# Who scales and shifts the last tile of H behind an inner norm: ScalarE or VectorE

## The chip, the cores and the metric

The kernel runs on one core of a Trainium2 chip (trn2). The metric is the device time of one execution in microseconds (us), as the median of several executions. Engines are called as the profile calls them: PE (TensorE; PEld are its weight loads), DVE (VectorE), ACT (ScalarE), POOL (GpSimd), SP (SyncE, which issues most of the loads).

## What is computed

One inference step of a backbone with two layers. Layer 0 mixes tokens by differential attention, layer 1 by a bidirectional mLSTM; each mixer is followed by a gated ConvFFN. 128 context tokens and 512 latent tokens go through together (640 columns), with 1024 features. Each of the four sub-layers ends in a post-norm, and the next sub-layer reads a modulated copy of its result. Cut to what matters here:

```python
def layer_norm(x, g, b):
    mu = jnp.mean(xf, axis=-1, keepdims=True)
    var = jnp.mean(jnp.square(xf - mu), axis=-1, keepdims=True)
    return (xf - mu) * lax.rsqrt(var + EPS) * g + b
def modulate(x, shift, scale):
    return x * (1 + scale) + shift
...
xs = post_norm(xs, mod_s[2] * ys, ln_g[i, 0], ln_b[i, 0])
hs = modulate(xs, mod_s[3], mod_s[4])
fs = conv_ffn(hs, ffn_w_up[i], ffn_conv_w[i], ffn_conv_b[i], ffn_w_down[i])
```

Shift and scale differ between context and latent tokens. Everything is float32.

## The kernel before, in words

Activations are kept feature-major: `X` holds 8 tiles (j = 0 to 7) of 128 features by 640 tokens. A float32 product is made of three products in fp32r: every operand is split into a high part (a cast) and a low part (the operand less its high part), and PE computes high·high, high·low of the weights, and low·high. So a tile of activations needs `Hh` (cast, by ACT) and `Hl` (subtraction, by POOL), and a unit of weights needs `whi` (ACT) and `wlo` (POOL).

The order on each engine is written out by hand, one program for each engine, and semaphores tie them together. There are three inner norms: norm 0 behind the attention's output projection, norm 1 behind the first ConvFFN, norm 2 behind the mLSTM's output projection. (The fourth, at the end, has no H behind it and isn't touched.) Around each of them:

- PE ends the statistics (`layer_norm_stats`, L658 to L668), and cannot go on until the first tile of H is there.
- DVE (`layer_norm`, L1728 to L1749) forms the variance, then for each j subtracts the mean (L1747) and multiplies by the reciprocal deviation (L1744), which leaves the normed `X[:, j]`, and raises `xn_ready`.
- ACT (`h_build`, L1142 to L1151) waits for `xn_ready`, computes gain times X plus bias into one of two buffers `h32[j % 2]` in two instructions (L1149: 128 columns with the context's `la` and `lb`, 512 with those of the latents), drains, and casts the buffer into `Hh[:, j]` (L1151), which raises `h_hi`. From j = 2 on it first waits for `h_ready`, that the low part of tile j - 2 has been made, so that its buffer is free.
- POOL (`h_lo`, L528 to L532) subtracts `Hh` from the buffer into `Hl[:, j]` and raises `h_ready`.
- PE (`first_pair`, L609 to L617, behind norms 0 and 2) runs, for each j, the high products of the first two weight units when `h_hi` has come (8 matmuls), and then the low ones when `h_ready` has come (4 matmuls). Behind norm 1 the place of the second unit is taken by the gates' columns (L920), also 12 matmuls for each j.

What follows on each engine: behind norms 0 and 2, DVE splits the third weight unit itself (`ffn`, L1765 `wnh` and L1767 `wnl`; `wnl` raises `w_lo`, for which SP waits before it loads the next unit into that buffer), behind norm 0 it also clears and fills `condf` (L1668, L1671), and then it starts the convolutions of the ConvFFN (L1753 to L1759). Behind norm 1 it fills two constants and two tiles of the identity (L1985 to L1989) and then waits for the gates. POOL goes on, behind norms 0 and 2, with the residual (L536) and the low parts of weights (L541). ACT empties the first two results (L1139) as soon as PE has ended them, and PE's third unit waits for the first of these copies.

Of the kernel before, what the change touches and what calls it, by code (L numbers as in the profile page):

```python
# [10 lines left out]
ALU = mybir.AluOpType  # L11
ACT = mybir.ActivationFunctionType
# [4 lines left out]
KT = D // P  # L17
# [56 lines left out]
LAST = KT - 1  # L74
# [13 lines left out]
SPANS = ((C0, C0 + CTX, 0), (L0, L0 + LAT, 1))  # L88
# [64 lines left out]
def hybrid_step(nc, a, o):  # L153

    ctx = ExitStack()
    with ctx:
        def sb(name, shape, dt=F32, scope=ctx):
            return scope.enter_context(nc.sbuf_tensor(name, shape, dt))
# [4 lines left out]
        def sem(name):  # L163
            return ctx.enter_context(nc.semaphore(name))


        X = sb("X", [P, KT, TP])
# [11 lines left out]
        la = sb("la", [P, KT, 2])  # L179
        lb = sb("lb", [P, KT, 2])  # L180
# [9 lines left out]
        h32 = [h32t[:, k, :] for k in range(2)]  # L190
# [125 lines left out]
        h32_ready, h_hi, h_ready = sem("h32_ready"), sem("h_hi"), sem("h_ready")  # L316
# [809 lines left out]
        def _(act):  # L1126
            fn = nc.scalar.activation
# [14 lines left out]
            def h_build(inst, n):  # L1142

                for j in range(KT):
                    act.wait_ge(xn_ready, KT * n + j + 1)
                    if j >= 2:
                        act.wait_ge(h_ready, KT * (n + 1) + j - 1)
                    for t0, t1, m in SPANS:
                        fn(h32[j % 2][:, t0:t1], X[:, j, t0:t1], ACT.Identity, scale=la[:, j, m:m + 1], bias=lb[:, j, m:m + 1])  # L1149
                    act.drain()  # L1150
                    nc.scalar.copy(Hh[:, j, :], h32[j % 2][:, :]).then_inc(h_hi, 1)  # L1151

            def square(n, j):
# [247 lines left out]
            acc_tiles(U_WO, 0, D, D, parted=True)  # L1401
            layer_norm(0)
            h_build(2, 0)
            ffn(0, U_FFN0, last=False)
            act.wait_ge(wg_in, 16)
            act.wait_ge(wg_clear, 1)
            for r, c in GCOL:
                last = nc.scalar.copy(wgh[:, :, r:r + 4], wgf[:, :, c:c + 4])
            last.then_inc(wgh_ready, 1)
            layer_norm(1)  # L1410

            h_build(3, 1)
            act.wait_ge(g_done, 1)
            fn(gr[0], mS[0:GR, :, 0:HALF], ACT.Identity, bias=gbias[0:GR, :])
# [210 lines left out]
            acc_tiles(U_MLOUT, 2, D, D, parted=True)  # L1625
            layer_norm(2)
            h_build(5, 2)
            ffn(1, U_FFN1, last=True)
            layer_norm(3)
# [9 lines left out]
        def _(dve):  # L1639
            tt, ts, stt = nc.vector.tensor_tensor, nc.vector.tensor_scalar, nc.vector.scalar_tensor_tensor  # L1640
# [87 lines left out]
            def layer_norm(n):  # L1728

                dve.wait_ge(va_done, n + 1)  # L1730
                dve.wait_ge(musq_ready, n + 1)
                sx2 = sx[:, 0:TP].rearrange("p (a b) -> p a b", a=2)
                stt(out=sx2, in0=rs[:, :, :], scalar=-1.0, in1=st_va[:, :, 0:HALF], op0=ALU.mult, op1=ALU.add)
                dve.drain()
                ts(sx[:, 0:TP], sx[:, 0:TP], 0.0, EPS, ALU.max, ALU.add).then_inc(var_ready, 1)
                if n == 3:
                    nc.vector.tensor_copy(ss[:, :].rearrange("p (a b) -> p a b", a=2), st_mu[:, :, 0:HALF]).then_inc(mur_ready, 1)
                tiles = KT if n < 3 else SIDE[0]
                for j in range(tiles + LEAD):
                    if j == LEAD:  # L1740
                        dve.wait_ge(rstd_psum, n + 1)
                    if j >= LEAD:
                        x = X[:, j - LEAD, :].rearrange("p (a b) -> p a b", a=2)
                        tt(x, x, st_va[:, :, 0:HALF], ALU.mult).then_inc(xn_ready, 1)  # L1744
                    if j < tiles:
                        x = X[:, j, :].rearrange("p (a b) -> p a b", a=2)
                        tt(x, x, st_mu[:, :, 0:HALF], ALU.subtract)  # L1747
                    if j > 0:
                        dve.drain()  # L1749

            def conv(c, f, tap, bias):

                ts(c[:, :], f[:, :], tap[1], bias, ALU.mult, ALU.add)  # L1753
                dve.drain()
                for t0, t1 in ((C0, L0), (L0, TP)):
                    stt(out=c[:, t0 + 1:t1], in0=f[:, t0:t1 - 1], scalar=tap[0], in1=c[:, t0 + 1:t1], op0=ALU.mult, op1=ALU.add)  # L1756
                dve.drain()
                for t0, t1 in ((C0, L0), (L0, TP)):
                    last = stt(out=c[:, t0:t1 - 1], in0=f[:, t0 + 1:t1], scalar=tap[2], in1=c[:, t0:t1 - 1], op0=ALU.mult, op1=ALU.add)  # L1759
                return last  # L1760
# [192 lines left out]
            for w in range(2):  # L1953
                dve.wait_ge(kv_out[w], 16 * DA_HEADS)
            layer_norm(0)
            ffn(0, U_FFN0)
            def gate_columns():
# [21 lines left out]
            for r, c in GCOL:  # L1979
                last = tt(wgl[:, :, r:r + 4], wgf[:, :, c:c + 4], wgh[:, :, r:r + 4].bitcast(F32), ALU.subtract)  # L1980
            last.then_inc(wg_ready, 1)
            layer_norm(1)


# [221 lines left out]
            coefficients((1, 0), mod(1, 3), mod(1, 4))  # L2206
            gated(U_MLOUT, NMOD + 2 * KT, True)
            layer_norm(2)
            dve.wait_ge(c_out, 32 * ML_HEADS)
            ffn(1, U_FFN1)  # L2210
# [97 lines left out]
```

## Time and profile before

| what | value |
|---|---|
| median of 3 executions | 1843.4 us (1843.14 to 1843.87) |
| the profiled execution, its own time | 1841.11 us |
| span of its trace | 1839.3 us |
| mean granted TensorE clock | 0.978 of full speed |
| PE busy | 1725.6 us, 94% of the span |
| PEld busy | 1613.5 us, 88% |
| DVE busy | 1050.2 us, 57% |
| ACT busy | 694.4 us, 38% |
| POOL busy | 642.7 us, 35% |

The span is what the trace covers; the execution's own time is 1.8 us more. Busy shares are averages over the whole program. In a timeline each row is one instruction, or a run of alike ones (x2), with its start in us from the span's start, its duration, its engine, its line in the kernel, the tiles written and read, and in brackets how long the engine was idle before and what ended that.

### The profile page before, as it was taken

The page shows a single profiled execution, that of the slowest core. Times are in us where ns is not written, and L with a number is a line of the kernel's source. Part 1 is how long each engine was busy: PE and PEld are TensorE (multiplying, and loading weights), DVE is VectorE, ACT ScalarE, POOL GpSimd, SP SyncE. Part 2 cuts the span into 40 slices and gives each one's busy share as a digit, 9 for nine tenths or more (in the row PEclk, how much of TensorE's full clock was granted, in tenths as well). Part 3 has the DMA queues.
Part 4 walks back from the last instruction along what each step waited for, and adds up shares of the span by engine and source line. Part 5 has one row for each costly group of instructions (what it writes and reads, how often), then busy time and mean ns, then how long its engine had stood idle before and what let it go on. Part 6 is the DMA issues. An engine that isn't in the chain of part 4 may idle for free.

```text
span 1839.3 us, 29894 instructions
## 1 busy us (share of the span) xinstructions
PE 1725.6 (94%) x11444; PEld 1613.5 (88%) x11444; DVE 1050.2 (57%) x1651; ACT 694.4 (38%) x1074; POOL 642.7 (35%) x292
## 2 busy tenths in 40 slices
PE   6899999788999999999978999997989999999996
PEld 3688888588988999899977999996979999999996
DVE  1277767755765614667337544544568881387823
ACT  3255555534423212322236544644253331133323
POOL 3312221335533333333435222222555333233444
PEclk8999999888999999999999999999999999999998
DMA  9722122111355223453211111110212222122221
GB/s 378 261 70 68 53 69 68 32 35 58 139 185 191 75 80 109 153 202 123 81 64 41 47 58 58 49 56 18 69 46 80 70 96 69 63 69 80 82 79 57
DMA packets 54034, 169.35 MB, mean 92 GB/s; under 512 B 7728, under 2 KB 13232, under 8 KB 53936
## 3 DMA queue, kind: packets, MB, share of 16 engines
q1 hardware_dynamic: 47600, 163.79, 26.0%
q10 hardware_dynamic: 6336, 4.20, 0.8%
q8 instruction: 69, 1.13, 0.3%
q14 instruction: 29, 0.24, 0.0%
HBM read 159.04 MB, written 4.72 MB: 89 GB/s over the span
## 4 chain that ended last, share of the span: by engine, by line
PE 82%; DVE 7%; ACT 4%; DVEq 2%; issue 2%; DMA 2%; POOL 1%; ACTq 0%; SPq 0%; POOLq 0%
PE pj L601 69%; PE mO L999 2%; DMA awr<-in_w_ada 2%; PE psO L777 2%; PE psS L742 1%; PE pfrow L626 1%; PE psT L758 1%; DVE pr L1856 1%; ACT pr L1260 1%; POOL X L549 1%; DVE sm L1841 1%; PE mS L955 1%; PE prow L626 1%; DVE h32t L1877 1%; PE mT L1024 1%
## 5 line engine op out<-in xcount | busy, mean ns | idle before, releaser
L472 POOL TENSOR_TENSOR wlo<-wraw,whi 128x1024 fp32r<-128x1024 f32 (+1 forms) x130 | 334.0, 2570 | 827.4 <-ACT whi L1134 827.4
L601 PE MATMUL pj<-Hh,whi 128*128 128x320 f32 x2400 | 569.7, 319 | 44.8 <-issue 13.7
L601 PE MATMUL pj<-Hh,wlo 128*128 128x320 f32 x2400 | 552.0, 312 | 0.0
L601 PE MATMUL pj<-Hl,whi 128*128 128x320 f32 x2400 | 546.3, 311 | 1.0 <-POOL Hl L502 1.0
L601 PEld LDWEIGHTS pj<-Hh,whi 128*128 128x128 f32 x2400 | 402.2, 190 | 76.8 <-issue 51.4
L601 PEld LDWEIGHTS pj<-Hh,wlo 128*128 128x128 f32 x2400 | 406.7, 190 | 0.0
L601 PEld LDWEIGHTS pj<-Hl,whi 128*128 128x128 f32 x2400 | 404.1, 190 | 1.3 <-POOL Hl L502 1.3
L1134 ACT CAST whi<-wraw 128x1024 fp32r<-128x1024 f32 (+1 forms) x180 | 199.4, 1108 | 314.2 <-PE pj L601 277.1
L1756 DVE SCALAR_TENSOR_TENSOR fcv<-fus,vec,fcv 128x127 f32<-128x127 f32 (+1 forms) x176 | 231.8, 1358 | 15.6 <-issue 15.6
L1711 DVE SCALAR_TENSOR_TENSOR X<-pj,mods,X 128x128 f32<-128x128 f32 (+1 forms) x144 | 54.5, 434 | 268.5 <-PE pj L601 268.2
L601 PE MATMUL pj<-Gh,wlo 128*128 128x320 f32 x704 | 160.4, 309 | 0.0
L601 PE MATMUL pj<-Gh,whi 128*128 128x320 f32 x704 | 160.4, 309 | 0.0
L601 PE MATMUL pj<-Gl,whi 128*128 128x320 f32 x704 | 160.3, 309 | 0.0
L1139 ACT COPY fus<-pj 128x640 f32<-128x640 f32 x88 | 60.7, 692 | 223.4 <-PE pj L601 223.2
L1759 DVE SCALAR_TENSOR_TENSOR fcv<-fus,vec,fcv 128x127 f32<-128x127 f32 (+1 forms) x176 | 123.6, 743 | 15.1 <-issue 15.1
L510 POOL TENSOR_TENSOR wlo<-wraw,whi 128x1408 fp32r<-128x1408 f32 (+2 forms) x28 | 83.9, 2995 | 105.5 <-ACT whi L1134 101.7
L601 PEld LDWEIGHTS pj<-Gl,whi 128*128 128x128 f32 x704 | 117.7, 188 | 0.0
L601 PEld LDWEIGHTS pj<-Gh,wlo 128*128 128x128 f32 x704 | 117.7, 188 | 0.0
L601 PEld LDWEIGHTS pj<-Gh,whi 128*128 128x128 f32 x704 | 117.6, 188 | 0.0
L1753 DVE TENSOR_SCALAR fcv<-fus,vec 128x640 f32<-128x640 f32 x88 | 58.8, 668 | 102.2 <-ACT fus L1139 102.1
L1218 ACT CAST Gh<-fpr 128x640 f32 (+1 forms) x44 | 32.0, 728 | 214.2 <-DVE fpr L1783 214.2
L541 POOL TENSOR_TENSOR wlo<-wraw,whi 128x1024 fp32r<-128x1024 f32 x24 | 59.2, 2470 | 126.6 <-ACT whi L1134 126.6
(306 smaller groups left out, 2046.2 us busy)
## 6 DMA issues: line engine op xcount, KB each, us to landing
wraw<-in_w_up SPq DMA_DIRECT2D x88, 512.0 KB, 3.3
fwr<-in_w_ada SPq DMA_DIRECT2D x56, 512.0 KB, 5.7
wraw<-in_w_dn SPq DMA_DIRECT2D x32, 704.0 KB, 4.0
awr<-in_w_ada SPq DMA_DIRECT2D x40, 512.0 KB, 10.3
wraw<-in_w_qkv SPq DMA_DIRECT2D x24, 512.0 KB, 3.5
wraw<-in_w_mlin SPq DMA_DIRECT2D x24, 512.0 KB, 3.2
sx<-h32t SPq DMA_DIRECT2D x128, 32.0 KB, 2.0
wraw<-in_w_wo SPq DMA_DIRECT2D x8, 512.0 KB, 3.3
```

The lines of the kernel that those rows point to most:

```text
L472: nc.gpsimd.tensor_tensor(wlo[k][:, 0:width], wraw[k][:, 0:width], whi[k][:, 0:width].bitcast(F32), ALU.subtract).then_inc(w_lo, 1)
L510: nc.gpsimd.tensor_tensor(wlo[k][:, c0:width], wraw[k][:, c0:width], whi[k][:, c0:width].bitcast(F32), ALU.subtract).then_inc(w_lo, 1)
L541: nc.gpsimd.tensor_tensor(wlo[v % 2][:, 0:width], wraw[v % 2][:, 0:width], whi[v % 2][:, 0:width].bitcast(F32), ALU.subtract).then_inc(w_l ...
L601: last = mm(out[:, c, 0:HALF], w, x[:, j, c * HALF:(c + 1) * HALF], start=(j == 0 and n == 0), stop=(j == n_k - 1 and n == 2))
L626: last = mm(out[g:g + 32, :], conds[:, 2 * kp + r, PAD - 2 * b:PAD - 2 * b + 32], bufs[u % len(bufs)][:, r, :], start=(b == 0 and kp < 2), ...
L777: last = mm(psO[:, :], v_[par][:, c, :], t_[:, c, :], start=(c == 0 and n == 0), stop=(c == 4 and n == 2))
L1134: nc.scalar.copy(whi[k][:, 0:width], wraw[k][:, 0:width]).then_inc(w_hi, 1)
L1139: nc.scalar.copy(dst.rearrange("p (a b) -> p a b", a=2), pj[k if pairs == 2 else 0][:, :, 0:HALF]).then_inc(pj_copied, 1)
L1711: last = stt(out=x, in0=pj[k][:, bank, c0:c1], scalar=gt, in1=x, op0=ALU.mult, op1=ALU.add)
L1753: ts(c[:, :], f[:, :], tap[1], bias, ALU.mult, ALU.add)
L1756: stt(out=c[:, t0 + 1:t1], in0=f[:, t0:t1 - 1], scalar=tap[0], in1=c[:, t0 + 1:t1], op0=ALU.mult, op1=ALU.add)
L1759: last = stt(out=c[:, t0:t1 - 1], in0=f[:, t0 + 1:t1], scalar=tap[2], in1=c[:, t0:t1 - 1], op0=ALU.mult, op1=ALU.add)
```

## The change

Behind each of the three inner norms, the scaling and shifting of the last tile (`LAST` = 7) is taken out of ACT's program and put into DVE's, behind the last multiplication of the norm. DVE waits for `h_ready` of tile 5, whose buffer `h32[1]` it overwrites, issues one tensor_scalar for each of the two spans, and raises the semaphore `h32_ready`, which existed and was not used. ACT waits for that in place of its two instructions and its drain, and casts as before.

```diff
                     if j >= 2:
                         act.wait_ge(h_ready, KT * (n + 1) + j - 1)
-                    for t0, t1, m in SPANS:
-                        fn(h32[j % 2][:, t0:t1], X[:, j, t0:t1], ACT.Identity, scale=la[:, j, m:m + 1], bias=lb[:, j, m:m + 1])
-                    act.drain()
+                    if j == LAST:
+                        act.wait_ge(h32_ready, n + 1)
+                    else:
+                        for t0, t1, m in SPANS:
+                            fn(h32[j % 2][:, t0:t1], X[:, j, t0:t1], ACT.Identity, scale=la[:, j, m:m + 1], bias=lb[:, j, m:m + 1])
+                        act.drain()
                     nc.scalar.copy(Hh[:, j, :], h32[j % 2][:, :]).then_inc(h_hi, 1)
...
                     if j > 0:
                         dve.drain()
+                if n < 3:
+                    dve.wait_ge(h_ready, KT * (n + 1) + LAST - 1)
+                    for t0, t1, m in SPANS:
+                        last = ts(h32[LAST % 2][:, t0:t1], X[:, LAST, t0:t1], la[:, LAST, m:m + 1], lb[:, LAST, m:m + 1], ALU.mult, ALU.add)
+                    last.then_inc(h32_ready, 1)
```

The instructions of DVE behind norm 0, before (wnh and wnl are the high and low part of the third weight unit, st_mu and st_va hold mean and reciprocal deviation):

```order
L1747 TENSOR_TENSOR X<-X,st_mu 128x640
L1744 TENSOR_TENSOR X<-X,st_va 128x640 x2
L1765 TENSOR_SCALAR wnh<-wraw 128x1024
L1767 TENSOR_TENSOR wnl<-wraw,wnh 128x1024
L1668 MEMSET condf 128x496
L1671 COPY condf<-cond 128x8x2
```

And now; the first of the two new ones waits for `h_ready`:

```order
L1747 TENSOR_TENSOR X<-X,st_va 128x640 x2
L1756 TENSOR_SCALAR h32t<-X,la,lb 128x128
L1756 TENSOR_SCALAR h32t<-X,la,lb 128x512
L1773 TENSOR_SCALAR wnh<-wraw 128x1024
L1775 TENSOR_TENSOR wnl<-wraw,wnh 128x1024
L1671 MEMSET condf 128x496
L1674 COPY condf<-cond 128x8x2
```

Everything behind the two new instructions, the split of the third unit first, now stands behind the wait for POOL's tile 5. The same engine behind norm 1, now (vc, gnb: constants; mKh, mKl: the identity's tiles), where the same two rows have come ahead of four that don't touch H:

```order
L1747 TENSOR_TENSOR X<-X,st_va 128x640 x2
L1756 TENSOR_SCALAR h32t<-X,la,lb 128x128
L1756 TENSOR_SCALAR h32t<-X,la,lb 128x512
L1993 MEMSET vc 128x2
L1994 MEMSET gnb 128x1
L1996 TENSOR_SCALAR mKh<-ident 128x128
L1997 TENSOR_SCALAR mKl<-ident 128x128
```

ACT's last tiles behind norm 0, before (fus: the first two results of PE on their way to the convolution):

```order
L1149 ACTIVATE h32t<-X,lb,la 128x128
L1149 ACTIVATE h32t<-X,lb,la 128x512
L1151 CAST Hh<-h32t 128x640
L1149 ACTIVATE h32t<-X,lb,la 128x128
L1149 ACTIVATE h32t<-X,lb,la 128x512
L1151 CAST Hh<-h32t 128x640
L1139 COPY fus<-pj 128x640 x2
```

And now:

```order
L1152 ACTIVATE h32t<-X,lb,la 128x128
L1152 ACTIVATE h32t<-X,lb,la 128x512
L1154 CAST Hh<-h32t 128x640 x2
L1139 COPY fus<-pj 128x640 x2
L1134 CAST whi<-wraw 128x1024
```

The two casts stand next to each other, with a wait for DVE between them. The orders of PE, POOL and SP are the same in both kernels.

## Rows read from the trace of the kernel before

**Rows 1.** The page: the chain that ended last, by engine.

```profile
PE 82%; DVE 7%; ACT 4%; DVEq 2%; issue 2%; DMA 2%; POOL 1%; ACTq 0%; SPq 0%; POOLq 0%
```

**Rows 2.** The chain in order of time: start, us, what; around norms 0 and 2.

```profile
444.12 6.92 issue
451.04 16.73 PE pj L601 x94
468.68 28.46 PE pj L601 x192
...
1349.58 16.35 PE pj L601 x94
```

**Rows 3.** Busy time and granted clock in two stretches of first_pair behind norm 0.

```profile
451.00:457.00 6.00, 5.96 (x22) 5.99 (x23) 5.70 (x9) 5.81 (x11) 4.99 (x4) 0.50 0.01 3
457.00:468.60 11.60, 11.05 (x75) 10.78 (x74) 7.14 (x8) 7.74 (x14) 9.16 (x6) 1.00 0.14 46
```

**Rows 4.** Timeline of weight loads (PEld) behind norm 0, tiles 6 and 7.

```profile
464.22 0.34 PEld L601 LDWEIGHTS pj<-Hh,whi 128*128 128x128 f32 x2
...
465.98 0.33 PEld L601 LDWEIGHTS pj<-Hh,whi 128*128 128x128 f32 x2
...
467.15 0.63 PEld L601 LDWEIGHTS pj<-Hl,whi 128*128 128x128 f32 x4
```

**Rows 5.** Timeline behind norm 0, the other engines, tiles 5 to 7 and after.

```profile
459.76 0.95 DVE L1765 TENSOR_SCALAR wnh<-wraw 128x1024 fp32r<-128x1024 f32 x1 [0.16 <-issue]
...
460.48 1.66 POOL L532 TENSOR_TENSOR Hl<-h32t,Hh 128x640 fp32r<-128x640 f32 x1 [0.33 <-ACT Hh L1151]
460.80 2.42 DVE L1767 TENSOR_TENSOR wnl<-wraw,wnh 128x1024 fp32r<-128x1024 f32 x1
...
462.24 1.20 ACT L1149 ACTIVATE h32t<-X,lb,la 128x128 f32<-128x128 f32 x2
462.38 3.80 POOL L532 TENSOR_TENSOR Hl<-h32t,Hh 128x640 fp32r<-128x640 f32 x2 [0.23 <-ACT Hh L1151]
463.25 0.33 SPq L363 DMA_DIRECT2D wraw<-in_w_up  x1
...
463.50 0.73 ACT L1151 CAST Hh<-h32t 128x640 fp32r<-128x640 f32 x1
...
467.84 1.29 ACT L1139 COPY fus<-pj 128x640 f32<-128x640 f32 x2 [3.61 <-PE pj L601]
468.74 0.61 DVE L1753 TENSOR_SCALAR fcv<-fus,vec 128x640 f32<-128x640 f32 x1 [4.05 <-ACT fus L1139]
```

**Rows 6.** Timeline of norm 1, tiles 6 and 7 and what follows.

```profile
976.53 1.56 POOL L532 TENSOR_TENSOR Hl<-h32t,Hh 128x640 fp32r<-128x640 f32 x1 [0.32 <-ACT Hh L1151]
...
977.62 0.73 ACT L1151 CAST Hh<-h32t 128x640 fp32r<-128x640 f32 x1
...
978.43 1.56 POOL L532 TENSOR_TENSOR Hl<-h32t,Hh 128x640 fp32r<-128x640 f32 x1 [0.34 <-ACT Hh L1151]
...
979.14 0.31 PEld L920 LDWEIGHTS mS<-Hh,wgh 128*100 128x100 f32 x2
...
980.31 0.32 PEld L920 LDWEIGHTS mS<-Hl,wgh 128*100 128x100 f32 x2
```

**Rows 7.** Timeline behind norm 2, tiles 6 and 7.

```profile
1360.92 3.83 POOL L532 TENSOR_TENSOR Hl<-h32t,Hh 128x640 fp32r<-128x640 f32 x2 [0.22 <-ACT Hh L1151]
...
1362.06 0.73 ACT L1151 CAST Hh<-h32t 128x640 fp32r<-128x640 f32 x1
...
1364.15 0.33 PEld L601 LDWEIGHTS pj<-Hh,whi 128*128 128x128 f32 x2
...
1365.32 0.63 PEld L601 LDWEIGHTS pj<-Hl,whi 128*128 128x128 f32 x4
```

**Rows 8.** The page: group of the convolutions' first instruction, with its idle time.

```profile
L1753 DVE TENSOR_SCALAR fcv<-fus,vec 128x640 f32<-128x640 f32 x88 | 58.8, 668 | 102.2 <-ACT fus L1139 102.1
```

**Rows 9.** Timeline of ACT: the next use of the buffer that SP reloads.

```profile
479.18 1.05 ACT L1134 CAST whi<-wraw 128x1024 fp32r<-128x1024 f32 x1
```

## The prediction

> **What bounds the kernel now.** I read the chain that ended last first, because the change can only pay where it touches that chain. PE holds 82% of it, ACT 4%, POOL 1% [rows 1]. Then the same chain in order of time around the norms. Behind norm 0 there is a gap of 6.92 us in which PE waits for the norm, and from 451.04 on the chain is PE alone for 16.73 us, until ACT empties the first result and PE goes on at 468.68; behind norm 2 the run is 16.35 us [rows 2]. ACT's work on H is in neither stretch. That is worth a question, since ACT needs about 1.9 us for a tile (two instructions 1.20 us, a gap of 0.06, the cast 0.73, less a small overlap [rows 5]), and PE less: its loads for tile 6 begin at 464.22 and those for tile 7 at 465.98, 1.76 us apart [rows 4]. PE is the faster one and still never waits for ACT. The granted clock says why: from 451 to 457 us it was 0.50 (1.2 GHz), from 457 on 1.00 (2.4 GHz) [rows 3], after the idle gap. In the slow stretch PE fell behind ACT, and in the five tiles that follow it doesn't catch up fully.
>
> The last view is the timeline at the last tile, where I compare when a part of H is there with when PE first loads weights for it. These differences are the slack that a faster or slower tile 7 meets:
>
> - Norm 0: the cast ends at 463.50 + 0.73 = 464.23 [rows 5], PE wants it at 465.98 [rows 4]: slack 1.75 us. The low part ends at 462.38 + 3.80 = 466.18 [rows 5], wanted at 467.15 [rows 4]: slack 0.97.
> - Norm 1: the cast ends at 978.35, wanted at 979.14: slack 0.79. Low part 979.99, wanted 980.31: slack 0.32 [rows 6].
> - Norm 2: the cast ends at 1362.79, wanted at 1364.15: slack 1.36. Low part 1364.75, wanted 1365.32: slack 0.57 [rows 7].
>
> All six are positive, so an earlier tile 7 gains nothing. What is left to ask is whether the change can make it later than the slack.
>
> **What leaves ACT.** Two instructions and a drain per norm: about 1.20 + 0.06 = 1.26 us [rows 5], three times. ACT then waits 3.61 us for PE before it copies the first result [rows 5], so this time only makes that wait longer. Value on the path: 0.
>
> **What comes to DVE.** Two tensor_scalar with per-partition operands, 128 and 512 columns. The nearest row is the convolution's, the same kind with 640 columns: 0.61 us [rows 5]. The pair handles the same 640 columns with a second start, so I take 0.75 us (bounds: 0.61, and twice that, 1.22). When do they start? POOL's tile 5 began at 460.48 and took 1.66 us [rows 5], 1.56 when nothing disturbs it [rows 6]. What disturbed it was wnh, which ran until 460.71 and now stands behind it, so `h_ready` comes near 462.04. With 0.10 us for the signal (ACT was released by the same event: 462.14, then 462.24 [rows 5]) the pair runs from 462.14 to about 462.9, the cast until about 463.7. Against 464.23 it is some 0.5 us earlier, into slack. Value: 0.
>
> **The shared resource.** DVE and POOL don't run side by side here. wnl, 1024 columns, was issued at 460.80 and took 2.42 us; POOL's tile 5 ended at 462.14, and wnl 1.08 us after that. In the other direction, POOL's tiles 6 and 7 took 3.80 us in place of 2 x 1.56 = 3.12: tile 6, issued at 462.38, got going only as wnl ended [rows 5]. So one stands still while the other runs, and the new pair falls just where POOL starts tile 6 (462.38). The second instruction, that of 512 columns, starts near 462.4 (the first one's share of 0.75 behind 462.14). There are two orders, and both are worked out:
>
> - *DVE first.* POOL's tile 6 waits until about 462.8 and ends near 464.3, wanted at about 465.4 (464.22 and the 1.17 us that lie between PE's first high and first low load of a tile, 465.98 to 467.15 [rows 4]). wnh waits for tile 6 too. If it then goes before POOL's tile 7 (0.56 us of its 0.95 were work: POOL's tile 4 ended 0.33 before 460.48, at 460.15, and wnh at 460.71 [rows 5]), tile 7 ends near 464.85 + 1.56 = 466.4, still ahead of 467.15. Norm 1: tile 6 ends near 978.4, tile 7, with the identity's tiles in between, near 980.2, ahead of 980.31 by a hair. Norm 2: near 1364.9, ahead of 1365.32. Cost: 0, with 0.1 or 0.2 us possible in norm 1.
> - *POOL first.* This is the rival below.
>
> The Trainium skill, SBUF — State Buffer, section Who interferes with whom, says that a VectorE tensor_scalar in a 2-port mode and a GpSimd instruction take an exclusive lock, that "whoever issues first gets the shared pair for the whole instruction", and that the other blocks. By it the 512-column instruction could stand a whole POOL tile behind, which speaks against this change; the trace agrees with the rule in the 2.42 us above, and the result would be the rival's time below and not mine.
>
> **What is moved behind the wait.** wnh and wnl. PE needs them, with the first result emptied, at 468.68 [rows 2]. Before they were done at 460.80 + 2.42 = 463.22. Now, with DVE first: tile 7 of POOL ends near 466.4, wnl 1.08 us later, near 467.5; with wnh behind tile 7 as well it is much the same. Slack left 1.2 us; norm 2 has about 0.9. Cost 0; if the cover went, PE would wait by as much as wnl is later than 468.68. SP's next load into that buffer goes out at 463.25 [rows 5], now near 467.5. ACT reads the buffer at 479.18 [rows 9], 11.7 us later, so 0. POOL's residual waits for the same semaphore and moves by 1.3 us; nobody waits for it there. The copy into condf and the residual may push the first convolution, 468.74 [rows 5], back by 0.3 us, or by some 1.5 where POOL's next split then gets in ahead. DVE has idle time for this: 102.2 us in front of 88 convolutions, 1.16 us each [rows 8], and PE's two result buffers lie between. Cost 0.
>
> **The sum.** 0 from ACT, 0 from the earlier tile, 0 from the moved split: 1841.11 + 0 for an execution like the profiled one. The profiled one was 2.3 us below the median of 1843.4, so one execution can lie that far off; I put the change, 0, on the median: 1843.4 us.
>
> **Rivals.**
> 1. *PE does wait for ACT.* The ends of matmuls are modelled, and if PE in truth kept step with ACT at full clock, the last tile's two instructions would come off the path. For: ACT's 1.9 us for a tile exceed PE's 1.76 [rows 4, 5]. Against: the six slacks. At most the 0.5 us by which the cast comes earlier in norm 0, and 0.73 where it follows the cast before it at once: 3 x 0.73 = 2.2 us, 1841.2 us.
> 2. *POOL takes tile 6 first* (slower). Place: between `h_ready` of tile 5 and the 512-column instruction. POOL's tile 6 runs from 462.38 to 463.94, then DVE's instruction until about 464.3, the cast until 465.0 (wanted 465.98, fine). But now wnh and wnl are issued at once behind it, from 464.3 to about 466.1, while POOL's tile 7 can only be issued at 465.1, after the cast. It waits and ends near 466.1 + 1.56 = 467.65, 0.5 us late. Norm 2 by the same steps: tile 6 to 1362.48, wnl to 1364.6, tile 7 to about 1366.1, 0.8 late. Norm 1 has no wnl, but the least slack: tile 6 to 978.09, cast to 979.25, tile 7 from 979.3 to 980.87, 0.56 late. Together 1.9 us: 1845.3 us. It decides when the 512-column instruction comes to the port after POOL's tile 6, a matter of 0.1 us. For: the two times, 462.4 and 462.38, can't be told apart by rows. Against: POOL's tile 6, issued at 462.38 with wnl until 463.22 in its way, lost 0.68 us and not 0.84, so it wants the port some 0.15 us after its start, which favours DVE.
> 3. *The late wnl starts a chain* (clearly slower). PE waits for wnl, and a late first convolution never catches up: one whole POOL tile more per ConvFFN norm, 2 x 1.56 = 3.1 us, with the 1.9 above 5.0 us, 1848.4 us. Against: 1.2 and 0.9 us of slack and DVE's idle time.
>
> That the change doesn't do what it says is excluded by the order of the instructions.
>
> **How the numbers follow.** My forecast 0.60; rival 2, in one or more norms, 0.28; rival 1 0.06; rival 3 0.03; 0.03 for what I don't see. The range takes in rival 2 and a little of rival 1, and the 0.7 us by which executions differ: 1841.6 to 1845.6 us. A measurement of this kernel tells about 0.2% (3.7 us) from no change. Forecast and rivals 1 and 2 are all within that; only rival 3 and unseen things lie outside: faster 0.02, same 0.94, slower 0.04.
>
> **What would show it.** Right: PE's run behind each norm has the length it had (16.7 and 16.4 us), ACT's last cast ends near 463.7 in norm 0's time, POOL's tile 6 is issued at the old place and takes about 0.4 us longer than 1.56, wnl ends before PE's third unit. Wrong: a gap in PE ahead of the low products of tile 7 (rival 2), a shorter run with the cast in the chain (rival 1), PE released by wnl (rival 3).

## The result, and the profile after

| | before | after |
|---|---|---|
| median of 20 executions each, us | 1842.3 (1839.26 to 1844.46) | 1844.61 (1840.31 to 1848.93) |
| ratio after / before, 95% | | 1.0016 [1.001, 1.0022] |
| the profiled execution, own time / span, us | 1841.11 / 1839.3 | 1840.64 / 1838.9 |
| mean granted clock in it | 0.978 | 0.979 |

The change costs 0.16%, some 2.9 us (0.0016 x 1842.3; by the interval 1.8 to 4.1; the two medians lie 2.3 us apart). That is inside the 0.2% that the prediction called "no change" and inside its range, but 20 executions of each kernel do tell it from nothing: it is slower. The forecast's own mechanism, a cost of 0, is wrong. The two profiled spans say the opposite (0.4 us shorter), so nothing can be read off a span here: in four executions of the unchanged kernel, norm 0 alone starts anywhere from 442.17 to 445.96 us, for reasons that lie ahead of it. (One of the 12 executions of the last run below, e8, took 2225.32 us at a mean granted clock of 0.715 and is left out of its ratio.)

The page after the change, its busy times and the shares of the chain that ended last:

```profile
PE 1722.8 (94%) x11444; PEld 1610.0 (88%) x11444; DVE 1052.9 (57%) x1657; ACT 691.3 (38%) x1068; POOL 642.7 (35%) x292
...
PE 79%; DVE 7%; ACT 5%; DVEq 3%; DMA 2%; POOL 2%; issue 2%; ACTq 1%; SPq 0%; POOLq 0%
```

ACT's busy time fell by 3.1 us, as the change says. DVE's rose by 2.7, but between two executions of the unchanged kernel it already differs by 2.2 (1050.2 and 1052.4). The shares of the chain (PE 82% before [rows 1]) say that something else than PE now stands in it. The chain in order of time, around norms 0, 1 and 2 (start, us, what), shows what:

```profile
458.31 1.59 POOL Hl L532
460.02 2.04 DVEq L1774
462.96 2.42 POOL Hl L532
467.20 28.45 PE pj L601 x192
...
973.15 1.58 POOL Hl L532
974.76 2.15 DVE h32t L1756 x2
977.81 1.57 POOL Hl L532
...
1357.70 1.59 POOL Hl L532
1359.46 2.01 DVEq L1774
1362.38 2.43 POOL Hl L532
1366.36 218.61 PE pj L601 x1488
```

Behind each norm PE's unbroken run [rows 2] is gone. In its place stand POOL's tile 5, then DVE (DVEq L1774 is DVE's queue, which stands at the drain between wnh and wnl while the new pair runs), then POOL's tile 7. The timeline behind norm 0, the rows that answer to [rows 5]:

```profile
458.31 1.58 POOL L532 TENSOR_TENSOR Hl<-h32t,Hh 128x640 fp32r<-128x640 f32 x1 [0.32 <-ACT Hh L1154]
...
459.92 2.13 DVE L1756 TENSOR_SCALAR h32t<-X,la,lb 128x128 f32<-128x128 f32 x2 [2.53 <-POOL Hl L532]
...
460.20 1.57 POOL L532 TENSOR_TENSOR Hl<-h32t,Hh 128x640 fp32r<-128x640 f32 x1 [0.31 <-ACT Hh L1154]
...
461.97 0.68 DVE L1773 TENSOR_SCALAR wnh<-wraw 128x1024 fp32r<-128x1024 f32 x1
...
462.16 0.73 ACT L1154 CAST Hh<-h32t 128x640 fp32r<-128x640 f32 x1 [2.04 <-DVE h32t L1756]
462.74 1.23 DVE L1775 TENSOR_TENSOR wnl<-wraw,wnh 128x1024 fp32r<-128x1024 f32 x1
462.94 0.56 PE L601 MATMUL pj<-Hh,whi 128*128 128x320 f32 x2 [0.20 <-ACT Hh L1154]
462.96 2.40 POOL L532 TENSOR_TENSOR Hl<-h32t,Hh 128x640 fp32r<-128x640 f32 x1 [1.20 <-ACT Hh L1154]
...
465.42 0.85 PE L601 MATMUL pj<-Hl,whi 128*128 128x320 f32 x4 [1.04 <-POOL Hl L532]
...
467.20 0.54 PE L601 MATMUL pj<-Hh,wnh 128*128 128x320 f32 x2 [0.92 <-ACT fus L1139]
```

Read from the top. DVE is released at 459.92, 0.03 us behind the end of POOL's tile 5 (459.89). Its pair then takes 2.13 us and ends at 462.05, while POOL's tile 6, issued at 460.20, takes an undisturbed 1.57 and ends at 461.77. Taken singly, the two instructions of the pair are

```profile
459.92 0.35 DVE L1756 TENSOR_SCALAR h32t<-X,la,lb 128x128 f32<-128x128 f32 x1 [2.53 <-POOL Hl L532]
460.18 1.87 DVE L1756 TENSOR_SCALAR h32t<-X,la,lb 128x512 f32<-128x512 f32 x1
```

So the 128-column instruction went first, POOL's tile 6 came between the two, and the 512-column one had to wait for it, although its row begins at 460.18 and POOL's at 460.20: *POOL first*, the second of the two orders that the prediction worked out. The cast is late (PE waits 0.20 for it); behind it wnl (462.74 to 463.97) is in the port as POOL's tile 7 is issued, and that takes 2.40 in place of 1.56. PE waits another 1.04 us for the low part.

**The measure for the runs.** As spans don't help, I measure each norm by itself: from the start of DVE's variance instruction (L1733, a SCALAR_TENSOR_TENSOR into sx, at 444.33, 958.48 and 1342.87 in the profile before; L1736 in the changed kernel) to the start of PE's next unit behind the norm. From this start on, what DVE, ACT and POOL do in one kernel repeats in every execution within 0.05 us. A plus sign, as in +20.0, counts from this start too. Call it S.

| | norm 0 | norm 1 | norm 2 | sum |
|---|---|---|---|---|
| before, the profiled execution | 24.35 | 24.92 | 24.00 | 73.27 |
| after, the profiled execution | 25.06 | 25.46 | 24.80 | 75.32 |

Here the change costs 0.71, 0.54 and 0.80 us, 2.05 together. (The clock behind norm 0 was not the same in these two executions; see b1 below.)

### The profile page after: what moved, and what is told of

Read it like the earlier page. It is cut to its first block, busy times and chain, and to the rows that moved or that the text cites. A ratio compares the mean times of both kernels' runs of the same rounds, so it can differ in the third digit from the quotient of the medians.

```text
span 1838.9 us, 29891 instructions
## 1 busy us (share of the span) xinstructions
PE 1722.8 (94%) x11444; PEld 1610.0 (88%) x11444; DVE 1052.9 (57%) x1657; ACT 691.3 (38%) x1068; POOL 642.7 (35%) x292
## 3 DMA queue, kind: packets, MB, share of 16 engines
q8 instruction: 69, 1.13, 0.3%
## 4 chain that ended last, share of the span: by engine, by line
PE 79%; DVE 7%; ACT 5%; DVEq 3%; DMA 2%; POOL 2%; issue 2%; ACTq 1%; SPq 0%; POOLq 0%
PE pj L601 66%; PE mO L999 2%; DMA awr<-in_w_ada 2%; PE psO L777 2%; PE pfrow L626 1%; PE psS L742 1%; DVE pr L1864 1%; PE psT L758 1%; ACT pr L1263 1%; POOL X L549 1%; DVE sm L1849 1%; ACT Hh L1154 1%; PE mS L955 1%; ACT h32t L1152 1%; POOL Hl L532 1%
```

## The experiments

The theory (A) is **the port**: POOL's tile 6 gets in ahead of the 512-column instruction, and wnl, now late, gets in ahead of POOL's tile 7. Rivals: **the clock** (B), that the changed kernel's TensorE clock falls more often or stays low for longer, and that this is the time; and **the held queue**, that what costs is wnh and wnl behind the wait for POOL's tile 5, whoever does the scaling.

**Both kernels again.** No edit; the kernel before, then the one after.

> The kernel before, once more, against itself: this shows what two equal kernels differ by. Both theories: ratio 1.000, interval about 0.001 wide. Theory A (the port: the 512-column tensor_scalar is held up by POOL's tile 6 in every execution) says nothing on this run. Theory B (the loss comes from the TensorE clock, which the change lets fall more often) expects the granted clock of this kernel to be near 0.978 in all executions. A second question it answers: how long PE runs at the 1.2 GHz level behind each norm in another execution. In the profiled execution of before it was about 6 us behind norm 0, in that of the change about 3 us.

> The changed kernel once more. Theory A: ratio 1.0016 within 0.0008, and in the trace the pair of tensor_scalar takes 2.1 us in all three norms and POOL's tile 7 is issued 2.75 to 2.8 us after its tile 6. Theory B: the same ratio, but a granted clock that lies lower than that of before by 0.002 or more in most executions, with the PE gaps of about 1 us as its cause.

Measured: before against itself 1.0002 [0.9993, 1.0011], so with 11 executions against the runs of before nothing under 0.09% is told. After against before 1.0011 [1.0002, 1.002], 2.0 us, slower again. S before 24.32, 24.90, 23.99 (73.21); after 25.09, 25.48, 24.81 (75.38). The cost stands in S a second time, 2.17 us. The mean clock of the executions was 0.9781 for before and 0.9766 for after: the clock as a rival keeps a foothold that this doesn't settle (see the last point on the prediction, below).

**What the pair of instructions costs when POOL doesn't block it (e1).** DVE reads its second operand from PSUM and multiplies with it, in place of adding the bias, so the shift of tile 7 is left out; three instructions, since the PSUM tile has two banks.

```diff
-                    for t0, t1, m in SPANS:
-                        last = ts(h32[LAST % 2][:, t0:t1], X[:, LAST, t0:t1], la[:, LAST, m:m + 1], lb[:, LAST, m:m + 1], ALU.mult, ALU.add)
+                    for (t0, t1), (bk, c0, c1), m in (((0, 128), (0, 0, 128), 0), ((128, 320), (0, 128, 320), 1), ((320, 640), (1, 0, 320), 1)):
+                        last = stt(out=h32[LAST % 2][:, t0:t1], in0=X[:, LAST, t0:t1], scalar=la[:, LAST, m:m + 1], in1=st_va[:, bk, c0:c1],
+                                   op0=ALU.mult, op1=ALU.mult)
```

> DVE's instructions for tile 7 read a PSUM operand (X times gain times the reciprocal deviation, without the shift: the shift of tile 7 is left out and its values differ), so they have one SBUF input and no two-port mode. Everything else as in the changed kernel. Theory A: the three instructions take 1.1 us together in place of 2.1, ACT's last cast begins 0.9 to 1.0 us earlier after POOL's tile 5, POOL's tile 7 ends about 1.5 us earlier, PE has no gap over 0.3 us ahead of tile 7's low products; ratio 1.000 within 0.0006. Theory B without A (it is the handing over between engines that leaves the gaps, not the port): the instructions still end about 2.1 us after POOL's tile 5 and the ratio stays at 1.0016. Theory C (the moved split of the third unit is what costs): instructions short, but POOL's tile 7 as late as before, ratio over 1.001.

The timeline of this run behind norm 0:

```profile
461.53 1.13 DVE L1756 SCALAR_TENSOR_TENSOR h32t<-X,la,st_va 128x128 f32<-128x128 f32 x3 [2.51 <-POOL Hl L532]
461.81 1.57 POOL L532 TENSOR_TENSOR Hl<-h32t,Hh 128x640 fp32r<-128x640 f32 x1 [0.32 <-ACT Hh L1154]
...
462.57 1.36 DVE L1774 TENSOR_SCALAR wnh<-wraw 128x1024 fp32r<-128x1024 f32 x1
462.77 0.73 ACT L1154 CAST Hh<-h32t 128x640 fp32r<-128x640 f32 x1 [1.03 <-DVE h32t L1756]
463.58 1.78 POOL L532 TENSOR_TENSOR Hl<-h32t,Hh 128x640 fp32r<-128x640 f32 x1 [0.19 <-ACT Hh L1154]
...
464.03 2.42 DVE L1776 TENSOR_TENSOR wnl<-wraw,wnh 128x1024 fp32r<-128x1024 f32 x1
```

The three instructions take 1.13 us beside POOL's tile 6, which takes its 1.57: neither stops the other. The cast comes 1.00 us earlier than in the changed kernel (19.02 in place of 20.02 us behind the norm's start), and now it is POOL's tile 7 that comes first and wnl that waits (2.42). S: 23.43, 25.47, 23.85 (72.75); ratio 1.0006 [0.9997, 1.0015]. With the same wait, the same work moved off ACT and the same place on DVE, but without the port, the cost in S is gone behind norms 0 and 2 (1.63 and 0.95 us less than after). Behind norm 1 S is what it is after, but there the clock rose late (after 5.0 us), and the kernel before has 25.50 with such a clock (b1), so this norm tells nothing. The other two speak for the port and against the held queue. The ratio by itself doesn't: its interval holds both 1 and the 1.0011 of after. The Trainium skill (SBUF — State Buffer, section Who interferes with whom) says that a VectorE instruction with at most one SBUF input, outside the 2-port modes, does not contend with GpSimd, while one with two SBUF inputs does with a GpSimd instruction that reads SBUF; this form (1.13 us) and wnl (2.42) agree with it by these rows.

**The wait alone (e4).** DVE waits for tile 5 and then goes on with wnh; ACT scales tile 7 as before.

```diff
-                    if j == LAST:
-                        act.wait_ge(h32_ready, n + 1)
-                    else:
-                        for t0, t1, m in SPANS:
...
                     dve.wait_ge(h_ready, KT * (n + 1) + LAST - 1)
-                    for t0, t1, m in SPANS:
-                        last = ts(h32[LAST % 2][:, t0:t1], X[:, LAST, t0:t1], la[:, LAST, m:m + 1], lb[:, LAST, m:m + 1], ALU.mult, ALU.add)
-                    last.then_inc(h32_ready, 1)
```

> The kernel before (ACT still scales and shifts tile 7) with nothing but DVE's wait for POOL's tile 5 put ahead of what follows the norm on DVE: the moved split alone. Counted from the start of the variance (L1733), as in all traces. Theory A (the loss is the pair standing still behind POOL's tile 6, and then wnl on tile 7) expects ACT's last cast at +19.2 as before; wnh comes to the port at +17.8, ahead of tile 6, and wnl waits for tile 6 or for both; POOL's tile 7 ends between +21.6 and +22.7; PE's third unit behind norms 0 and 2 begins at +24.4 and +24.0 as before, or up to 0.3 later; ratio 1.000 to 1.0004. Theory C (the moved split is what costs): third unit at +25.0 and +24.8, ratio over 1.001.

```profile
463.81 0.69 DVE L1767 TENSOR_SCALAR wnh<-wraw 128x1024 fp32r<-128x1024 f32 x1 [2.51 <-POOL Hl L532]
...
464.09 4.36 POOL L532 TENSOR_TENSOR Hl<-h32t,Hh 128x640 fp32r<-128x640 f32 x2 [0.31 <-ACT Hh L1151]
...
464.60 2.42 DVE L1769 TENSOR_TENSOR wnl<-wraw,wnh 128x1024 fp32r<-128x1024 f32 x1
...
468.50 0.85 PE L601 MATMUL pj<-Hl,whi 128*128 128x320 f32 x4 [0.20 <-POOL Hl L532]
```

wnh, released at once, is in the port ahead of POOL's tile 6, and wnl (2.42 us) waits for tile 6 and then stands in front of tile 7: both tiles take 4.36 us, 1.24 above 2 x 1.56, where they took 3.80 before. S 23.95, 25.78, 23.98 (73.71), ratio 0.9999 [0.999, 1.0008]. The moved split by itself makes POOL 0.56 us later than before. Against the profile of before the sum of S is 0.44 us longer, but norm 1 alone is 0.86 longer, where no DVE instruction of this edit is in POOL's way (its clock rose late there, after 5.7 us). Norm 2, at the same clock as before, is unchanged (23.98 and 24.00); behind norm 0, at a clock between those of the executions of before (4.0 us), S lies between theirs and PE waits 0.20 us. So the held queue explains a few tenths behind norm 0 at most, not 2 us.

**wnl held back (e7).** The changed kernel; wnl waits until POOL's tile 7 is done, so only the second collision goes.

```diff
+                dve.wait_ge(h_ready, KT * (2 * layer + 2))
```

> The changed kernel, with wnl held back until POOL has made the low part of tile 7, so that it can't stand in its way. Theory A: the pair of tensor_scalar is as slow as before (2.13 us) and the last cast starts at +20.0, but POOL's tile 7 takes 1.57 us in place of 2.42 and ends at +22.4 in place of +23.2; PE's third unit begins at +24.3 to +24.4 behind norm 0 and +24.0 to +24.2 behind norm 2 (in place of 25.06 and 24.80), norm 1 stays at +25.46; ratio about 1.0005. If tile 7 still takes 2.4 us, wnl isn't what held it.

```profile
462.93 2.14 DVE L1756 TENSOR_SCALAR h32t<-X,la,lb 128x128 f32<-128x128 f32 x2 [2.51 <-POOL Hl L532]
463.21 1.58 POOL L532 TENSOR_TENSOR Hl<-h32t,Hh 128x640 fp32r<-128x640 f32 x1 [0.32 <-ACT Hh L1154]
...
465.99 1.58 POOL L532 TENSOR_TENSOR Hl<-h32t,Hh 128x640 fp32r<-128x640 f32 x1 [1.20 <-ACT Hh L1154]
467.60 1.23 DVE L1776 TENSOR_TENSOR wnl<-wraw,wnh 128x1024 fp32r<-128x1024 f32 x1 [1.92 <-POOL Hl L532]
467.62 0.85 PE L601 MATMUL pj<-Hl,whi 128*128 128x320 f32 x4
```

The first collision is unchanged (2.14), the second is gone: POOL's tile 7 takes 1.58, not 2.40. S 24.23, 25.47, 23.97 (73.67); ratio 1.0000 [0.9991, 1.0009]. Norms 0 and 2 get 0.83 us each back, norm 1, which has no wnl, nothing. The ratio's interval ends below that of the result (1.001), though it overlaps that of a0 (from 1.0002). So 1.7 us of the cost hang on wnl's place, behind a cast that the first collision has made late; the 0.5 us of norm 1 is the first collision alone.

**A third buffer (e2, and with wnl held e6).** Tile 7 goes to `sx`, which is free there, so that DVE needs no wait. In lines that the cut leaves out, ACT's cast and POOL's subtraction read `sx` for this tile, and ACT doesn't wait for tile 5 either; e6 adds e7's line.

```diff
-                    dve.wait_ge(h_ready, KT * (n + 1) + LAST - 1)
...
-                        last = ts(h32[LAST % 2][:, t0:t1], X[:, LAST, t0:t1], la[:, LAST, m:m + 1], lb[:, LAST, m:m + 1], ALU.mult, ALU.add)
+                        last = ts(sx[:, t0:t1], X[:, LAST, t0:t1], la[:, LAST, m:m + 1], lb[:, LAST, m:m + 1], ALU.mult, ALU.add)
```

> DVE writes tile 7 into a buffer of its own (sx, free at that time), so it waits for nobody, and neither ACT nor DVE waits for POOL's tile 5. ACT casts tiles 6 and 7 one behind the other. Theory A: DVE's pair falls beside POOL's tiles 4 and 5 and is done before ACT needs it, whoever has the port; POOL's tile 7 follows tile 6 at once and ends some 0.35 us earlier than in the kernel before, wnh and wnl stand where they stood or up to 1.5 us later; ratio 0.9995 to 1.0000 (3 x 0.35 = 1.0 us at most where PE keeps up with ACT). Theory B: about 1.000 too, as PE's gaps go. Theory C: over 1.001 if wnl falls on POOL's tile 7.

> A buffer of its own for tile 7 and wnl held back behind POOL's tile 7: what both findings suggest. Theory A: POOL's tiles 6 and 7 follow each other without hindrance and tile 7 ends at +21.2 to +21.3 in all three norms (before: 21.84, 21.51, 21.87). PE's third unit: no earlier than before where the clock stays at 1.2 GHz for over 5 us behind the norm (24.3 and 24.0), 0.3 to 0.6 earlier where it rises sooner. Ratio 0.9995 to 1.0003, which 5 rounds will hardly tell from 1.

The timeline of e2 behind norm 0:

```profile
459.30 1.58 POOL L532 TENSOR_TENSOR Hl<-h32t,Hh 128x640 fp32r<-128x640 f32 x1 [0.32 <-ACT Hh L1154]
...
460.39 1.03 DVE L1755 TENSOR_SCALAR sx<-X,la,lb 128x128 f32<-128x128 f32 x2
...
461.34 2.06 DVE L1772 TENSOR_SCALAR wnh<-wraw 128x1024 fp32r<-128x1024 f32 x1
...
463.50 2.43 DVE L1774 TENSOR_TENSOR wnl<-wraw,wnh 128x1024 fp32r<-128x1024 f32 x1
...
464.80 2.56 POOL L532 TENSOR_TENSOR Hl<-sx,Hh 128x640 fp32r<-128x640 f32 x1
```

The pair takes 1.03 us, and that isn't its size either: POOL's tile 4 runs until 460.88, and the 128-column instruction, issued at 460.39, takes 0.57 in place of 0.35. Unhindered the two take 0.35 (after) and 0.55 (e5 below), and their rows overlap by 0.08 or 0.09, so the pair is 0.81 us by itself. The last cast starts 17.88 us behind the norm's start (before: 19.17), yet POOL ends tile 7 at +22.3 (before +21.84) behind norms 0 and 2, since it and wnl collide again; that is not the earlier end that was expected. Behind norm 1, where there is no wnl, it ends at +21.15 (before +21.51). S of e2 24.65, 24.81, 23.97 (73.43), ratio 1.0006 [0.9997, 1.0015]; of e6, whose tile 7 takes 1.55 and ends at +21.31, 23.79, 25.87, 23.98 (73.64), ratio 1.0004 [0.9995, 1.0013]. An H that is ready 0.5 us earlier than before gives nothing that these runs can tell. (The high values of norm 1 in e4 and e6, 25.78 and 25.87, go with the latest clocks, 5.7 and 5.9 us.)

**The 512 columns first (e5).** The same two instructions in the other order; one execution.

```diff
-                    for t0, t1, m in SPANS:
+                    for t0, t1, m in SPANS[::-1]:
```

> The changed kernel with the two instructions of the pair in the other order. Theory A (whoever comes first has the port until its instruction ends): the 512-column one starts 0.03 us after POOL's tile 5, ahead of tile 6, and runs unhindered (about 0.5 us); POOL's tile 6 then goes and is itself 0.1 to 0.4 us longer than 1.57; the 128-column one waits for its end: the pair ends near +20.0 to +20.2, and the last cast starts no earlier than in the changed kernel (+20.0). If the port went to the shorter or to DVE by right, the pair would take 0.8 us and the cast start at +18.7.

```profile
463.57 2.06 DVE L1756 TENSOR_SCALAR h32t<-X,la,lb 128x512 f32<-128x512 f32 x2 [2.51 <-POOL Hl L532]
463.85 1.70 POOL L532 TENSOR_TENSOR Hl<-h32t,Hh 128x640 fp32r<-128x640 f32 x1 [0.31 <-ACT Hh L1154]
465.55 0.68 DVE L1773 TENSOR_SCALAR wnh<-wraw 128x1024 fp32r<-128x1024 f32 x1
...
466.54 2.41 POOL L532 TENSOR_TENSOR Hl<-h32t,Hh 128x640 fp32r<-128x640 f32 x1 [0.99 <-ACT Hh L1154]
```

The two instructions of the pair singly:

```profile
463.57 0.55 DVE L1756 TENSOR_SCALAR h32t<-X,la,lb 128x512 f32<-128x512 f32 x1 [2.51 <-POOL Hl L532]
464.03 1.60 DVE L1756 TENSOR_SCALAR h32t<-X,la,lb 128x128 f32<-128x128 f32 x1
```

This shows the step by itself. Now the long instruction (0.55 us, unhindered, until 464.12) holds the port when POOL's tile 6 comes at 463.85, and tile 6 takes 0.13 us longer (1.70). And then POOL takes the port, *between* DVE's two instructions, and the short one waits: the pair still takes 2.06. The port is let go at the end of each instruction, and POOL, which stands waiting, has it before the next of a pair that follows at once.

From these rows comes an estimate of when each engine wants the port, counted from the start of its row. POOL's tile 6 lost 0.13 of the 0.27 us that lay between its start and 464.12: it wanted the port some 0.14 after its start (0.14 to 0.16 over the three norms). The blocked 128-column instruction ended 0.08 us behind POOL (465.55 to 465.63) and takes 0.35 alone: 0.27 of it was done before. The blocked 512-column one in the changed kernel ended 0.28 us behind POOL (461.77 to 462.05) and takes 0.55 alone: again 0.27. So in the changed kernel DVE's 512 columns wanted the port at 460.18 + 0.27 = 460.45 and POOL's tile 6 at 460.20 + 0.15 = 460.35. By this estimate POOL was 0.10 us ahead, though its row starts 0.02 us behind. S 24.98, 25.39, 24.73 (75.10), about that of the changed kernel; its one time, 1847.64 us at a mean clock of 0.972, is within what single executions of the changed kernel show (up to 1848.93).

**Three more executions of both kernels (b1, b2, a1).** No edit, one execution each.

> One more look at the kernel before, for the stretch from the start of the variance (L1733) to PE's third unit, by how long the granted clock stays at 1.2 GHz after PE's restart. Theory: where it stays 5 to 6 us behind norm 0 the stretch is 24.3 us, as in both traces so far; where it rises within 3 us PE catches up with POOL's tile 7 (which ends at +21.84) and the stretch is 23.4 to 23.9 us, so that the change costs 1.2 us or more there and not 0.7. ACT, DVE and POOL keep their times within 0.05 us either way.

> As the look before it: the stretch behind norm 0 is 24.3 us with 5 to 6 us of 1.2 GHz and 23.4 to 23.9 with 3 us; behind norm 1 24.9 with under 4 us and 25.5 to 25.9 with 5 us and more, as the two experiments with long stretches of 1.2 GHz behind norm 1 show; behind norm 2 24.0 with 5 us and 23.4 to 23.9 with less.

> One more look at the changed kernel. Theory: since PE waits for POOL's tile 7 behind all three norms, the stretch is 25.06 to 25.10, 25.46 to 25.48 and 24.80 us whatever the clock does, unless the 1.2 GHz last for more than 5 us behind norm 1 (then up to 25.9 there). The pair of tensor_scalar takes 2.13 to 2.15 us, POOL has the port first in all three.

S of norm 0 in e1 (23.43) was below that of before, and these show why. Times 1842.67, 1839.50 and 1842.98 us. S of before was 23.64, 25.50, 23.88 (73.02) in b1 and 23.64, 25.38, 23.85 (72.87) in b2: the kernel before doesn't have one S, as I had taken it. That of after was 25.03, 25.46, 24.80 (75.29), the same a third time. The granted clock (the column ahead of the last two) in b1 behind norm 0, where PE begins at 451.85:

```profile
452.00:455.00 3.00, 3.00 (x12) 3.00 (x13) 2.85 (x5) 2.87 (x6) 2.67 (x2) 0.50 0.00 0
455.00:458.00 3.00, 3.00 (x22) 3.00 (x21) 2.85 (x5) 2.94 (x6) 2.36 (x3) 1.00 0.02 5
```

It rose to 2.4 GHz 3.1 us after PE's restart; in the profile of before it did so after 5.96 [rows 3]. Then PE isn't behind POOL at all. The timeline of b1:

```profile
463.19 3.82 POOL L532 TENSOR_TENSOR Hl<-h32t,Hh 128x640 fp32r<-128x640 f32 x2 [0.22 <-ACT Hh L1151]
...
465.54 0.85 PE L601 MATMUL pj<-Hl,whi 128*128 128x320 f32 x4 [0.28 <-POOL Hl L532]
...
467.26 0.63 PEld L601 LDWEIGHTS pj<-Hl,whi 128*128 128x128 f32 x4
```

In the kernel before, too, PE waits for a low part at norm 0, 0.28 us here and 0.43 in b2. It is that of tile 6, which wnl delays: tile 6 ends at 465.49, and tile 7 at 467.01, 0.25 us before PE's load for it. Over all profiled executions, PE's time at 1.2 GHz after these gaps was 2.9 to 6.0 us, whatever the kernel. All of them, S and in brackets the us at 1.2 GHz after PE's restart:

| | norm 0 | norm 1 | norm 2 |
|---|---|---|---|
| before | 24.35 (6.0) | 24.92 (3.8) | 24.00 (5.1) |
| b0 | 24.32 (5.9) | 24.90 (3.7) | 23.99 (5.1) |
| b1 | 23.64 (3.1) | 25.50 (5.1) | 23.88 (4.9) |
| b2 | 23.64 (2.9) | 25.38 (4.8) | 23.85 (4.8) |
| after | 25.06 (3.0) | 25.46 (3.5) | 24.80 (4.7) |
| a0 | 25.09 (6.0) | 25.48 (3.1) | 24.81 (5.0) |
| a1 | 25.03 (3.4) | 25.46 (3.9) | 24.80 (4.9) |
| e1, PSUM operand | 23.43 (3.0) | 25.47 (5.0) | 23.85 (4.8) |
| e4, wait alone | 23.95 (4.0) | 25.78 (5.7) | 23.98 (5.1) |
| e7, wnl held | 24.23 (4.2) | 25.47 (4.9) | 23.97 (4.8) |
| e2, third buffer | 24.65 (6.0) | 24.81 (3.5) | 23.97 (5.1) |
| e6, both | 23.79 (4.1) | 25.87 (5.9) | 23.98 (5.1) |
| e5, 512 first | 24.98 (4.0) | 25.39 (4.6) | 24.73 (5.7) |
| e8, before with wnl held | 23.08 (3.0) | 25.39 (4.8) | 23.86 (4.8) |

That lets like be compared with like. At norm 0 with a late rise (5.9 to 6.0 us), before has 24.32 and 24.35 and after 25.09: 0.74 to 0.77. With an early one (2.9 to 3.1), before has 23.64 and after 25.06: 1.42. At norm 2 the difference is 0.80 to 0.95. At norm 1 it is 0.54 to 0.58 where the clock rose after 3.1 to 3.9 us in both. Where before's rose after 4.8 or 5.1 us (25.38 and 25.50) it is 0.1 or nothing: e7 is the changed kernel behind norm 1, since its edit touches only wnl, and has 25.47 with a rise after 4.9. The clock thus sets how much of a late H is seen. Before's S follows it; after's S, set by POOL, does not.

What PE waits for these low parts behind norms 0 and 2 is also in one row of the groups by line (after the second bar: the idle time, the part put down to POOL's L532, and that put down to another stage's L502, the larger first). In b1, then in a0, then in the profile after:

```profile
L601 PE MATMUL pj<-Hl,whi 128*128 128x320 f32 x2400 | 547.5, 312 | 1.3 <-POOL Hl L502 1.0 <-POOL Hl L532 0.3
```

```profile
L601 PE MATMUL pj<-Hl,whi 128*128 128x320 f32 x2400 | 547.3, 311 | 1.8 <-POOL Hl L502 1.0 <-POOL Hl L532 0.8
```

```profile
L601 PE MATMUL pj<-Hl,whi 128*128 128x320 f32 x2400 | 546.1, 311 | 2.8 <-POOL Hl L532 1.8 <-POOL Hl L502 1.0
```

0.3 us before, with the early rise; 0.8 after with the late rise at norm 0 and 1.8 with the early one.

**Before, with wnl held (e8).** Whether the collision of wnl and POOL's tiles is worth taking out of the kernel before.

```diff
                 dve.drain()
+                dve.wait_ge(h_ready, KT * (2 * layer + 2))
```

> The kernel before with wnl held back until POOL has made the low part of tile 7: is there something to gain from the same collision in the kernel before, where wnl stands in the way of tile 6? POOL's tile 7 ends at +21.55 in place of 21.84 behind norms 0 and 2. Where the clock stays at 1.2 GHz for 5 us nothing is gained, elsewhere up to 0.3 us per norm: ratio 0.9997 to 1.0000, not to be told from 1. If it gained more, wnl would hold more than this tile.

POOL's tiles 6 and 7 behind norm 0 take 1.58 and 1.57, tile 7 ends at +21.54 in place of +21.84, wnl comes behind it, and PE waits less than 0.1 us for a low part at norm 0. S 23.08, 25.39, 23.86 (72.33), the shortest of all, 0.56 us less at norm 0 than b1 at nearly the same clock (3.0 and 3.1 us), more than the 0.3 that was expected: in b1 PE waits for tile 6, which wnl delays too. The ratio is 0.9998 [0.9989, 1.0007]: half a microsecond is below what these runs tell. It is no version that I can call better.

## Why the prediction was wrong, step by step

- **What leaves ACT is worth nothing.** Right as far as the runs tell. e1 and e6 keep this part of the change and have tile 7's low part ready 0.2 and 0.5 us earlier than before, and neither is faster. (e1's shorter S behind norm 0, 23.43, goes with a tile 6 that wnl no longer delays; behind norm 2, at the same clock, it has 23.85 like b2.)
- **The pair takes 0.75 us.** Nearly right: 0.81 us unhindered (0.35 and 0.55 less the overlap of 0.09), between the bounds of 0.61 and 1.22. With POOL in its way 2.13.
- **When it starts.** I took 0.10 us for the signal behind POOL's tile 5, from ACT; DVE was released after 0.03. That brought DVE 0.07 us forward, and still did not put it ahead.
- **"*DVE first.*" This is the step that failed.** The sentences were "The second instruction, that of 512 columns, starts near 462.4 (the first one's share of 0.75 behind 462.14)" and, against the rival, that POOL "wants the port some 0.15 us after its start, which favours DVE". The start was right: 462.4 is 0.26 behind 462.14, and measured it is 0.26 behind the first one's (459.92 to 460.18). POOL's 0.15 was right too (e5: 0.14 to 0.16). What failed is that POOL got such a delay and DVE none, as if a row's start were the moment at which DVE takes the port. By the blocked rows a tensor_scalar of this kind wants it 0.27 us after its start (an estimate, worked out at e5). In all nine norms of the three traces of the changed kernel the row of the 512 columns starts 0.02 to 0.03 us ahead of POOL's tile 6, and in all nine POOL got in: its tile 6 took 1.57 or 1.58 us, where DVE first would have made it some 2.0. That DVE takes the port late is read from rows and no run varies it by itself; that POOL goes between the two instructions is shown. I gave *DVE first* 0.60 and the rival 0.28, though I had written that 462.4 and 462.38 "can't be told apart by rows".
- **Rival 2's working.** It holds almost row by row. It had the last cast end at 465.0 on the clock of the profile before (measured +20.75 behind 444.33: 465.08), POOL's tile 7 issued at 465.1 (465.15) and ended at 467.65 (+23.22: 467.55). It summed 0.5 + 0.56 + 0.8 = 1.9 us; S shows 0.71 to 0.77, 0.54 to 0.58 and 0.80 to 0.82 in the first two pairs of executions, 2.05 and 2.17 together. Its 0.5 for norm 0 is to be held against 0.74 to 0.77, where both clocks rose as late as in the rows it was worked out from. Its time, 1845.3 us, would be 1.9 above before; the runs have 2.9 [1.8 to 4.1] and 2.0 above.
- **"All six are positive."** The slack was read from one execution, whose clock rose late behind norm 0 (5.96 us). In b1 and b2, with an early rise, the 0.97 us of tile 7's low part are 0.25 and 0.24, and tile 6's low part has no slack: PE waits 0.28 or 0.43 us for it. It is why the cost may exceed rival 2's: with the early rise at norm 0 the sum would be 1.42 + 0.55 + 0.8 to 0.95, 2.8 to 2.9 us, an estimate put together from several executions; b1 and b2, whose clock rose late behind norm 1, lie 2.3 and 2.4 us below a1.
- **The moved split.** Right as to PE, which never waited for wnh or wnl, but I looked only at who needs wnl, and gave it 0. It costs as a user of the port: 0.83 us at each of norms 0 and 2 (e7). In my chosen order it stood behind POOL's tile 7, so the failed step carried this one with it.
- **Rival 1** (PE waits for ACT) and **rival 3** (a chain that starts at wnl) did not happen. The first convolution behind norm 0 starts with ACT's copy, as before.
- **The clock** is not needed for S, which is longer by 2.0 to 2.5 us through waits for POOL at known places. For the whole time it stays open. Of 31 executions of the changed kernel (the result and a0), 9 have a mean granted clock of 0.972 to 0.975 and take 1847.0 us on average. Of 88 of the kernel before (b0 and those measured beside the later runs), none is below 0.976. At 0.978 in both, 5 of the changed kernel average 1843.5 and 45 of before 1842.4, 1.1 us apart, less than the 2.0 of S (five executions make this rough). So a part of the measured 2.0 to 2.9 us may come with the clock. No run shows why some executions of the changed kernel have the lower one.

## What to carry to other kernels

Before moving work between engines, ask who else uses what the new engine shares, and treat two instructions back to back as two requests: what waits gets in between. A short first instruction on a shared port can leave the long one a whole instruction of the other engine behind. Where the order hangs on 0.1 us, the starts of two rows don't decide it: estimate for both engines how long after its start each wants the port, from rows in which it was blocked. And a slack read in one trace behind an idle gap of PE is a slack at that execution's clock; take it from several, or assume an early rise of PE's clock.

## What the runs showed of the hardware

- DVE and POOL hand the port over between two instructions of DVE that follow each other at once: in the three norms of e5 and the nine of the changed kernel.
- By estimate from blocked rows, a tensor_scalar with two per-partition operands wants the port 0.27 us after its row's start, POOL's tensor_tensor about 0.15 (after, e5).
- Unhindered, such a tensor_scalar in float32 takes 0.35 us for 128 columns, 0.55 for 512 (after, e5) and 0.61 for 640 [rows 5]: the short one is far more than a fifth.
- A scalar_tensor_tensor with its second operand in PSUM and POOL's tensor_tensor don't hold each other up: 1.13 us for three beside 1.57 (e1).
- DVE came 0.03 us behind the event of POOL that released it, where ACT took 0.10.
- After an idle gap of the same length at the same place, PE ran at 1.2 GHz for 2.9 to 6.0 us in one and the same kernel (b2, before); what DVE, ACT and POOL did in that stretch repeated within 0.05 us.
